# Gate-a projection of a hybrid decoder layer as Strassen pairs, with the DeltaNet output blocks in one row

## What is computed

```python
xn = rms_norm(h, norm1)
proj = xn @ w_in
q, k, v, z, b_raw, a_raw, sc_c, sc_u, sc_b, gate_a, gate_b = split_columns(proj, PROJ_WIDTHS)
...
y_a = o.reshape(bsz, seq_len, DN_WIDTH).astype(h.dtype) @ w_dn_out
y_b = (sc_b * causal_depthwise_conv(sc_c * sc_u, conv_sc)) @ w_sc_out
mixed = jax.nn.sigmoid(gate_a) * y_a + jax.nn.sigmoid(gate_b) * y_b
h = h + mixed @ w_o
gt, up = jnp.split(rms_norm(h, norm2) @ w_gate_up, 2, axis=-1)
return h + (jax.nn.silu(gt) * up) @ w_down
```

## Time and profile before

| | us |
|---|---|
| median of 3 runs | 1044.33 (1044.2 to 1044.61) |
| the profiled execution | 1044.56 |
| its span, first to last instruction | 1042.7 |
| PE busy | 1029.3 (99%) |
| PE weight loads busy | 925.2 (89%) |
| DVE busy | 637.1 (61%) |
| ACT busy | 487.3 (47%) |
| POOL busy | 471.3 (45%) |

### The profile page before, as it was taken

One profiled execution on the slowest core, in us unless ns is written; L12 is line 12 of the kernel. 1 busy time (PEld: TensorE's weight loads), 2 busy tenths in 40 slices (PEclk: granted clock), 3 DMA queues, 4 the chain that ended last, 5 costly groups with the idle time before them and its releaser, 6 DMA issues.

```text
span 1042.7 us, 22625 instructions
## 1 busy us (share of the span) xinstructions
PE 1029.3 (99%) x9025; PEld 925.2 (89%) x9025; DVE 637.1 (61%) x1141; ACT 487.3 (47%) x1069; POOL 471.3 (45%) x403
## 2 busy tenths in 40 slices
PE   9999999999999999999999999999999999999996
PEld 8989899999999998978888888889999999988886
DVE  6575766757665757573321112599999999972103
ACT  7735444453545353642422333565555555653322
POOL 0163636354454536362554555652222222455553
PEclk9999999999999999999999999999999999999999
DMA  6222222222222122112253233223333332332312
GB/s 230 73 74 75 79 62 75 64 88 63 79 68 80 63 87 68 62 63 77 86 182 118 84 101 102 95 68 101 103 121 96 109 109 97 122 108 93 102 61 81
DMA packets 28825, 95.61 MB, mean 92 GB/s; under 512 B 2984, under 2 KB 5288, under 8 KB 28720
## 3 DMA queue, kind: packets, MB, share of 16 engines
q1 hardware_dynamic: 27520, 91.77, 27.0%
q10 hardware_dynamic: 1200, 2.38, 0.7%
HBM read 92.03 MB, written 2.11 MB: 90 GB/s over the span
## 4 chain that ended last, share of the span: by engine, by line
PE 91%; DVE 5%; ACT 2%; issue 1%; DMA 0%; DVEq 0%; ACTq 0%
PE bank L1392 90%; DVE og_lo L1231 1%; DVE pair_sums L1252 1%; DVE w_lo L1255 1%; DVE cv L1081 0%; DVE og_lo L1224 0%; DMA h_in<-gc_dram 0%; PE bank L1586 0%; PE bank L1592 0%; ACT w_hi L534 0%; DVE h L1202 0%; DVE raw L910 0%; DVE c L1270 0%; DVE bank L1212 0%; DVE t L1217 0%
## 5 line engine op out<-in xcount | busy, mean ns | idle before, releaser
L433 POOL TENSOR_TENSOR w_lo<-w_raw,w_hi 128x512 fp32r<-128x512 f32 x202 | 274.2, 1371 | 342.0 <-ACT w_hi L534 341.9
L1392 PE MATMUL bank<-x_hi,w_hi 128*128 128x258 f32 (+2 forms) x896 | 247.6, 334 | 0.2 <-DVE raw L910 0.2
L1392 PE MATMUL bank<-x_hi,w_lo 128*128 128x258 f32 (+2 forms) x896 | 230.5, 315 | 0.0
L1392 PE MATMUL bank<-x_lo,w_hi 128*128 128x258 f32 (+2 forms) x896 | 228.0, 315 | 0.0
L534 ACT ACTIVATE w_hi<-w_raw 128x512 fp32r<-128x512 f32 x278 | 166.7, 622 | 90.5 <-PE bank L1392 86.7
L1392 PEld LDWEIGHTS bank<-x_hi,w_lo 128*128 128x128 f32 x896 | 147.3, 189 | 11.1
L1392 PEld LDWEIGHTS bank<-x_hi,w_hi 128*128 128x128 f32 x896 | 146.3, 189 | 11.8 <-DVE raw L910 0.3
L1392 PEld LDWEIGHTS bank<-x_lo,w_hi 128*128 128x128 f32 x896 | 146.3, 189 | 8.8
L1392 PE MATMUL bank<-og_hi,w_hi 128*128 128x256 f32 (+1 forms) x416 | 124.4, 299 | 1.4 <-DVE w_lo L1255 1.0
L1392 PE MATMUL bank<-xe,w_hi 128*128 128x256 f32 (+1 forms) x602 | 123.2, 293 | 0.8 <-DVE w_lo L1255 0.7
L1392 PE MATMUL bank<-og_hi,w_lo 128*128 128x256 f32 (+1 forms) x416 | 124.0, 298 | 0.0
(11 more groups left out here) (306 smaller groups left out, 1828.1 us busy)
## 6 DMA issues: line engine op xcount, KB each, us to landing
w_raw<-w_stream SPq DMA_DIRECT2D x140, 512.0 KB, 3.5
cst<-w_stream SPq DMA_DIRECT2D x22, 512.0 KB, 3.5
h_in<-h_t SPq DMA_DIRECT2D x4, 528.0 KB, 7.1
h<-h_t ACTq DMA_DIRECT2D x1, 2048.0 KB, 11.7
h_in<-gc_dram SPq DMA_DIRECT2D x7, 264.0 KB, 3.0
out<-h SPq DMA_DIRECT2D x4, 256.0 KB, 2.9
out<-h SPq DMA_DIRECT2D x2, 384.0 KB, 2.6
cst<-consts SPq DMA_DIRECT2D x1, 512.0 KB, 8.8
```

The lines of the kernel that those rows point to most:

```text
L433: nc.gpsimd.tensor_tensor(low_weights(n)[:, at], raw_weights(n)[:, at], high_weights(n)[:, at].bitcast(f32), ALU.subtract).then_inc(wlo_re ...
L1392: return nc.tensor.matmul(o, w, x, start=start, stop=stop)
```

## The change

The eight `ga` blocks no longer alternate with the `dn` blocks. The order is `ga` 0 to 7, `dn` 0 to 7, `wo` 0 to 7. Two `ga` blocks form a pair and take the seven products of the gate/up pairs, with the same slots and banks; the pairs are counted through (`PAIRS` = 4 + 22). The sums of tokens that this needs are made from the normalised input during blocks 65 to 68 (`x_sums_made` on DVE, `x_sums_high` on ACT). Each gate has its own buffer, in memory that is free by then. The load of `h1`, whose memory these buffers overlap, moves from behind block 66 to the first `dn` block. `evacuate` of a `dn` block is as before, but for the gate's buffer. The diff, cut, in the order of the file (tables and waits; then POOL, ACT, DVE and PE):

```diff
-BLOCKS += [("ga", 0)] + [x for m in range(KT - 1) for x in (("ga", m + 1), ("dn", m))] + [("dn", KT - 1)]
-BLOCKS += [("wo", m) for m in range(KT)]
+BLOCKS += [(kind, m) for kind in ("ga", "dn", "wo") for m in range(KT)]
...
+X_SUMS_FROM = GA - 7
...
-ON_POOL = [0, 1, 2, 6] + [NP * m + i for m in range(1, FT) for i in (3, 6)]
+FIRST_FF = NP * GATE_PAIRS
+ON_POOL = [0, 1] + [NP * g + i for g in range(GATE_PAIRS) for i in (3, 6)]
+ON_POOL += [FIRST_FF + i for i in (0, 1, 2, 6)] + [NP * g + i for g in range(GATE_PAIRS + 1, PAIRS) for i in (3, 6)]
...
         def wait_weights_free(engine, n, half):
...
+            elif DN <= n < DN + 2:
+                engine.wait_ge(prod_done, FIRST_FF - 4 + 2 * (n - DN) + half + 1)
...
             for n in range(FFN):
+                if n == GA:
+                    for p in ON_POOL[2:ON_POOL.index(FIRST_FF)]:
+                        part_low(p)
+                    split_weights(DN, 0)
+                    split_weights(DN, 1)
+                if n in PAIR_OF:
+                    continue
...
+            def x_sums_high(k):
+                for i in range(2):
+                    act.wait_ge(xs_made, 2 * k + i + 1)
+                    copy(xs_hi[:, 2 * i:2 * i + 2, k, :], halves_of(dbank[2 + i][:, :])).then_inc(xs_high, 1)
+            def gate_sigmoid(m):
+                act.wait_ge(gate_scaled, gate_number("ga", m) + 1)
+                nc.scalar.activation(ga_gate[m], ga_gate[m], ACT.Sigmoid, scale=-1.0 if m % 2 else 1.0).then_inc(ge_ready, 1)
...
+            def gate_pairs():
+                part_high(2)
+                for g in range(GATE_PAIRS):
+                    p = NP * g
+                    part_high(p + 3)
+                    if g:
+                        gate_sigmoid(2 * g - 2)
+                    copy_first(g)
+                    part_high(p + 4)
+                    part_high(p + 5)
+                    if g:
+                        gate_sigmoid(2 * g - 1)
+                    part_high(p + 6)
+                    for i in range(3):
+                        if g < GATE_PAIRS - 1:
+                            part_high(p + 7 + i)
+                        elif i < 2:
+                            split_weights(DN, i)
...
-                if n == AT["gb", 5]:
-                    act.wait_ge(oglo_ready, HEADS)
+                if X_SUMS_FROM <= n < X_SUMS_FROM + 4:
+                    x_sums_high(n - X_SUMS_FROM)
+                if n == DN:
+                    gate_sigmoid(KT - 2)
+                    gate_sigmoid(KT - 1)
+                    act.wait_ge(prod_done, FIRST_FF)
                     act.dma_start(h1[:, :, :], h_t[:, :, META:L]).then_inc(h_again, 16)
...
-                    mult(ybf, p[0][:, :], gates[i % 2]).then_inc(dn_gated, 1)
+                    mult(ybf, p[0][:, :], ga_gate[m]).then_inc(dn_gated, 1)
...
+            def x_sums_made(k):
+                fa, fb = gate_a, ga_gate[0]
+                a, b = slice(0, QUARTER), slice(QUARTER, T)
+                s12, s34 = dbank[2], dbank[3]
+                tokens = slice(META, L)
+                nc.vector.tensor_tensor(fa[:, :], x_hi[:, k, tokens].bitcast(f32), x_lo[:, k, tokens].bitcast(f32), ALU.add)
+                link(nc.vector.tensor_tensor(fb, x_hi[:, k + 4, tokens].bitcast(f32), x_lo[:, k + 4, tokens].bitcast(f32),
+                                             ALU.add))
+                link(nc.vector.tensor_tensor(s12[:, a], fa[:, a], fa[:, b], ALU.subtract))
+                link(nc.vector.scalar_tensor_tensor(s12[:, b], fb[:, b], -1.0, s12[:, a], ALU.mult, ALU.subtract))
+                nc.vector.scalar_tensor_tensor(s34[:, b], s12[:, b], -1.0, fb[:, a], ALU.mult, ALU.subtract).then_inc(xs_made, 1)
+                nc.vector.tensor_tensor(s34[:, a], fb[:, b], fa[:, b], ALU.subtract).then_inc(xs_made, 1)
+                for i in range(2):
+                    dve.wait_ge(xs_high, 2 * k + i + 1)
+                    nc.vector.tensor_tensor(xs_lo[:, 2 * i:2 * i + 2, k, :], halves_of(dbank[2 + i][:, :]),
+                                            xs_hi[:, 2 * i:2 * i + 2, k, :].bitcast(f32), ALU.subtract).then_inc(xs_low, 1)
+            def gate_scale(m):
+                dve.wait_ge(joined, join_number(m // 2, "c21" if m % 2 else "c12"))
+                x = gate_c2 if m % 2 else halves_of(tg[:, :])
+                mult(halves_of(ga_gate[m]), x, halves_of(rs1[:, META:L])).then_inc(gate_scaled, 1)
+            def gate_pairs():
+                part_low(2)
+                weight_sum(0, "s4")
+                part_low(4)
+                part_low(5)
+                for g in range(GATE_PAIRS):
+                    p = NP * g
+                    if g:
+                        weight_sum(g, "s3")
+                        join(g - 1, "c21")
+                        weight_sum(g, "s4")
+                        gate_scale(2 * g - 1)
+                        part_low(p + 4)
+                        part_low(p + 5)
+                    join(g, "v")
+                    join(g, "w")
+                    if g < GATE_PAIRS - 1:
+                        weight_sum(g + 1, "s1")
+                    if g:
+                        dve.wait_ge(gate_scaled, gate_number("ga", 2 * g - 2) + 1)
+                    join(g, "c11")
+                    if g < GATE_PAIRS - 1:
+                        part_low(p + 7)
+                    if g:
+                        dve.wait_ge(gate_scaled, gate_number("ga", 2 * g - 1) + 1)
+                    join(g, "uc22")
+                    if g < GATE_PAIRS - 1:
+                        weight_sum(g + 1, "s2")
+                        part_low(p + 8)
+                    join(g, "c12")
+                    if g < GATE_PAIRS - 1:
+                        part_low(p + 9)
+                    gate_scale(2 * g)
+                join(GATE_PAIRS - 1, "c21")
+                gate_scale(KT - 1)
...
             for n in range(FFN):
...
+                if n == GA:
+                    for _ in chores:
+                        pass
+                    gate_pairs()
+                if n in PAIR_OF:
+                    continue
...
+                if X_SUMS_FROM <= n < X_SUMS_FROM + 4:
+                    if n == X_SUMS_FROM:
+                        dve.wait_ge(oglo_ready, HEADS)
+                    x_sums_made(n - X_SUMS_FROM)
+                if n == GA - 1:
+                    for name in ("s1", "s2", "s3"):
+                        weight_sum(0, name)
...
+            def gate_pairs():
+                pe.wait_ge(xs_low, 8)
+                for g in range(GATE_PAIRS):
+                    for i, name in enumerate(FACTORS):
+                        if g or i == 6:
+                            wait_bank_free(g, i)
+                        elif i >= 4:
+                            wait_result_read(pe, *BLOCKS[GA - 6 + i])
+                        part_product(NP * g + i, name, {})
...
+                if n == GA:
+                    gate_pairs()
+                if n in PAIR_OF:
+                    continue
+                if DN <= n < DN + 2:
+                    pe.wait_ge(joined, join_number(GATE_PAIRS - 1, "w"))
+                else:
                     wait_result_read(pe, *BLOCKS[n - 2])
```

## The result

The changed kernel takes 1048.07 us (median of 6 runs, 1047.57 to 1048.25), the kernel before 1044.26: ratio 1.0035, with a 95% interval of 1.0022 to 1.0048. It is slower by 3.8 us; the forecast was 1048.7.

What follows compares the result with a forecast made beforehand. PE, busy for 99% of the span, was taken to bound the kernel. The terms -5.0 + 5.3 + 1.1 + 2.5 + 0.4 = +4.3 us gave a forecast of 1048.7 us, range 1045.5 to 1052.

Steps and rivals of the forecast that it cites:

- The pairs: ga blocks as four pairs: 9.91 us of matmuls each in place of 11.17, a gain of 5.0 us.
- product 2: In the pairs, DVE's low part meets POOL's and PE waits: 0.4 us, bounds 0 and 2.0.
- The dn chain: Adjacent dn blocks: a 6.67 us cycle through POOL's yb_lo against 5.58 stalls dn4 to dn7 and wo0, 5.3 us.
- Tile 7 of wo0: In wo0, DVE's last yb_lo ends after tile 7 needs it: 1.1 us, bounds 0.5 and 1.3.
- The token sums: Sums in the gb/sc blocks meet POOL and stall blocks 68 and 70 by 1.1 and 1.4 us: 2.5 us.
- Covered at no cost: The moved h1 load, from dn0 on, and dn0's weights, ready 0.7 us early, cost nothing.
- The second one: Rival: dn cycle under 5.58 us, so dn blocks follow unhindered and it is faster, 1040 to 1042 us; chance 0.06.
- The first, sums hidden: Rival: token sums stall nothing, the dn chain costs 6.4 us and gives back the gain, 1045.7 to 1046; chance 0.2.
- The third, DVE behind in the pairs: Rival: DVE falls behind in the pairs, or sums stall at each block, 1051 to 1054 us; chance 0.12.

Runs made afterwards that it cites:

- the adds out of PSUM: Changed kernel, with ACT copying the low parts of the normalised input into PSUM, so the token sums' two adds have one SBUF input: 1047.71 us.
- POOL's order: Changed kernel, with POOL making yb_lo of a dn block between the two low halves of the next block's weights instead of behind both: 1040.77 us.
- the last group moved: Kernel with adds out of PSUM, product 2 on POOL and yb_lo between weight halves, plus last token sums moved from behind block 68 to 69: 1039.30 us.
- the two buffers: Changed kernel, with dn results going by turns into two buffers, so DVE waits for yb_lo of two blocks before; POOL keeps its order: 1041.28 us.
- three mended: Changed kernel with adds of the token sums out of PSUM, low part of product 2 on POOL, and yb_lo between the weight halves: 1039.68 us.

## Why the prediction came out right

**The pairs.** -5.0 was predicted for the matmuls, with 0.4 for product 2. From ga0 to dn0 40.14 us were measured against 39.6 + 0.4. The stall at product 2 is 0.56 us and has the cause that was named; without it a pair takes 9.86 us, 0.05 less than from the earlier trace rows.

**The dn chain.** The cycle of 6.67 us, read off the only two adjacent `dn` blocks, is the measured spacing to 0.03 us, and the first stall is ahead of dn4, as worked out. The row is 5.1 us longer than eight blocks of 5.58, where 5.3 was predicted. By the experiments the chain costs more, 5.8 us, for an undisturbed row takes 43.95 us and not 44.65 (last section): five cycles of 6.65 against blocks of 5.49. That 5.1 is so near 5.3 is in part luck, for the quicker pace of PE gave back 0.7 us that no term had. This is also why the kernels that mend it came out 0.4 and 0.9 us below what was expected of them.

**Tile 7 of wo0.** 1.1 predicted, 1.2 measured, released by DVE's last `yb_lo`.

**The token sums.** 2.5 predicted, 1.9 measured: stalls at the two blocks that were named, 0.76 and 0.97 us in place of 1.1 and 1.4. The layout by hand had the second group meet POOL, as it does. From the start of block 65 (516.02) the scaling of gb5 comes at 13.9 us, where 14.1 was worked out, and that of gb6 at 26.3 in place of 27.0. The first stall was mis-added: the terms named behind 14.1 give 17.3 and not 17.6, and 17.6 against 16.7 is 0.9 and not 1.1; measured, PE starts block 68 at 17.5. The second is 0.4 us too dear: the weights come at 29.7 where 30.4 was worked out, and PE is there 0.2 us earlier. The prediction also names the low parts among what meets POOL; they read one operand from PSUM, and two take 1.29 us (520.17) beside POOL's halves (518.24, 2.93 us). The reason given, two SBUF inputs beside POOL, is shown by the adds out of PSUM: 0.68 in place of 1.79 us at the same place. The Trainium skill (SBUF — State Buffer, section Who interferes with whom) states that a DVE instruction with at most one SBUF input, outside its modes that use two ports, doesn't contend with GpSimd. These runs agree, with 0.68 us for such adds, and the operation behind with two SBUF inputs took 1.47 us in place of 0.43.

**Covered at no cost.** The h1 load and the weights of dn0 stall nobody: PE goes from the last product (597.04) to dn0 (597.16) without a gap.

**The rivals.** The second one (faster, if `yb_lo` goes ahead of a half of the weights) was made by the experiment with POOL's order: 1040.77, where 1040 to 1042 had been worked out. Its condition, a cycle under one block, was stricter than needed: 5.67 us against 5.49 did it for eight blocks. The first, sums hidden, did not come: the stage to ga0 took 52.08 us, and only with the adds out of PSUM and the last group moved did it take 50.15. The third, DVE behind in the pairs, did not come: with 38.2 of 40.1 us busy DVE kept ahead of PE.

## What to carry to other kernels

When blocks of one kind are brought together, look for the longest cycle (a chain of waits that closes on itself) over the engines through the single buffer that they share, and compare it with one block, not with the block and its neighbour: busy shares of 22, 29 and 54% hid a bound of 6.67 us against 5.5. What such a row costs is mended by the order on one engine, here `yb_lo` ahead of one half of the weights (1048.07 became 1040.8 us, and 1039.3 with the two smaller stalls mended), so a change that gains on PE and loses on a helper should be tried with that order before it is dropped. A stall taken away ahead of a stage with a full helper has to be followed to the end of that stage, since another outcome of a meeting for memory gave 1.3 us back.

## What the runs showed of the hardware

**Two paces of PE at one clock.** A matmul 512 wide follows the one before by 0.233 us in most blocks ahead of the changed ones and by 0.229 in others, both at a granted clock of 1.00. In the kernel before, the `ga` and `dn` blocks run at 0.233 and `wo`, from its second or third block on, at 0.229; in the changed kernel the `dn` row runs at 0.229 already. With the two buffers all of `wo` and with three mended most of it is at 0.233 again, which costs 0.8 us of the stage. PE in order of time, in `wo` of the kernel with two buffers and of the one with POOL's order:

```profile
659.64 0.40 PE L1547 MATMUL bank<-yb_hi,w_lo 128*128 128x512 f32 x1
...
661.04 0.40 PE L1547 MATMUL bank<-yb_hi,w_lo 128*128 128x512 f32 x1
```

```profile
659.62 0.39 PE L1547 MATMUL bank<-yb_hi,w_lo 128*128 128x512 f32 x1
...
660.99 0.39 PE L1547 MATMUL bank<-yb_hi,w_lo 128*128 128x512 f32 x1
```

Six steps take 1.40 us in the one and 1.37 in the other. What sets the pace stays open; it was not tried.

**A meeting costs the wait for the other's instruction.** DVE's adds took 0.68 us alone and 1.77 to 1.79 beside POOL in the changed kernel, where POOL's operation takes 1.30; two meetings follow each other when POOL has the next operation queued. Which engine goes first hung on 0.1 us at product 2 (POOL 558.45, DVE 558.56), and again at DVE's second weight sum (POOL 679.92, DVE 680.01), 140 us behind the edit, where it moved the gate/up stage by 1.3 us.
